# A hybrid decoder layer on one core: pair products taken from rows as loaded, the residual input loaded by feature, and a tile's preparation spread over more half-jobs

## The chip, the cores and the metric

The kernel runs on 1 core of one Trainium2 chip. The metric is the device time of one execution in microseconds (us), as the median of several runs of the same program. The text writes PE for TensorE, DVE for VectorE, ACT for ScalarE, POOL for GpSimd and SP for SyncE; PEld is the weight load that PE does beside its matmuls, and SPq in a row is SP's own sequencer.

## The reference

One inference step of a one-layer decoder, for a prompt of 1024 tokens and for 8 sequences of 4 sample tokens (32 rows), model width 1024, all float32:

```python
h = rmsnorm(x, g_mix); proj = h @ w_in                       # q|k|v, z, b, a, glu
qkv = silu(causal_depthwise_conv(qkv_full, w_short))         # 4 taps
q = l2norm(heads(q)); k = l2norm(heads(k))                   # 8 heads x 64
# chunks of 64 tokens: L = strict(k_beta k^T * decay), T = (1 + L)^-1
# u = T v_beta, w = T (k_beta e^gc), qk = (q k^T) * decay, then a scan over chunks
o, s_new = gated_delta_rule(q, k, v, g, beta, s0)
o = rmsnorm(o, g_o) * silu(heads(z))
cv = silu(group_layernorm(depthwise_conv31(glu)))            # 31 taps
x = x + concat([o, cv]) @ w_out
x = x + square(relu(rmsnorm(x, g_mlp) @ w_up)) @ w_down
x = x + (p_emb @ w_ple) * sigmoid(rmsnorm(x, g_ple) @ w_ple_gate)
y = rmsnorm(x, g_final)                                      # also: new states
```

## The kernel before, in words

The tokens are worked on in two halves: half 0 holds 512 prompt tokens in one piece, half 1 holds 512 prompt tokens and the 32 sample rows in two pieces of 256 and 288 columns. Activations lie by feature (128 features on the partitions, tokens along the free axis). Every large product is a list of **jobs** (plan, L82): one job makes one block of 128 output features. A weight block of up to 128x1024 is loaded by SP, ACT makes its high part (split_hi, L939) and DVE its low part (split_lo, L1656), three buffers deep, and PE does three matmuls for every 128 input features, high by high, low by high and high by low (L1318). The order of jobs is: input projections of half 0, those of half 1, then for half 0 the 8 `out` jobs, 8 groups of 4 `up` jobs and 8 short `down` jobs each, and 8 pairs of `gate` and `ple`; then the same for half 1. There the groups are longer.

Each job is issued in two **half-jobs**. `schedule` (L150) hangs every other piece of work behind one half-job as a stage, and every engine works through its own instructions strictly in that order; a stage of DVE that comes late holds up all that stands behind it on DVE, and PE waits for whatever it needs. The helper `adv(h, k)` goes forward from half-job h by about k units of a full half-job's PE time; the half-jobs of a `down` job in half 0 count half a unit.

The delta rule works on **tiles** of 128 tokens, t = 0..3 in half 0, 4..7 in half 1, t = 8 the sample rows. `prep` (L167) hangs five stages on half-jobs:

- `dk`: POOL makes products of gate logs and a triangle (`ug`, L893), PE turns them into decay exponents, ACT takes exp (Dm, L1114).
- `tok`: PE transposes the tile of q, k and v (`qt`, loaded from `qkv_dram`) to token rows (12 matmuls, L1406), ACT squares q and k (L1108), DVE sums the squares (L1858).
- `sc`: ACT makes the norms (L943, L1120, each after a table load), DVE five small scale factors (L1870 to L1874) and then evicts seven 128x512 products (L1878): tk[0..3], Kbe, Kd and Vb.
- `bk`: PE transposes tk[0..3] back to features (16 matmuls, L1419) and ACT copies them out (L1129) as KTl, RR twice, and QdT.
- `pr`: PE multiplies the chunks' keys with keys and queries (64 small matmuls, L1430), DVE masks the decays (L1885) and writes LQ (L1889), SP stores its key part to `lt_dram`.

After four tiles `lp` loads the pair matrices (Lp, L769), DVE inverts them by columns (L1903, L1904) and the scan over 8 chunks follows. Taps of the 31-wide convolution (`tap`, L1984) fill DVE between the stages, by a fill level that `conv` works out.

The residual input x comes in rows (xr, xrs; `load_rows`, L785 to L795, five loads issued together for each half): an `out` job ends with PE transposing 128x128 blocks of it into the job's PSUM accumulation (`residual`, L1294 to L1303), and ACT reads the PSUM three times (L1007 to L1009: xT, the input of the next product, and the square).

Of the kernel before, what the change touches and what calls it, by code (L numbers as in the profile page):

```python
# [13 lines left out]
P = 128  # L14
# [135 lines left out]
def schedule():  # L150
# [156 lines left out]
    put(max(scan_end, o0 - 4), "xr", 0)  # L307
# [7 lines left out]
    put(h, "dk", NT)  # L315
    put(h, "tok", NT)
    for what in ("sc", "bk", "pr"):
        h = adv(h)
        put(h, what, NT)
# [30 lines left out]
    put(o1 - 10, "xr", 1)  # L350
# [5 lines left out]
    conv(0, lambda p: half("ga", 0, p // 2 * 2 + 1) + 3, half("ga", 1, 2) - 2)  # L356
# [27 lines left out]
SEVEN = uses({"vec": 1, "abt": 1, "ge": 1, "dk": 1, "bk": 1, "uw": 1, "got": 1, "hq": 3})  # L384
# [41 lines left out]
def seg(t):  # L426
    return 0 if t < HT else 1
# [11 lines left out]
def build(nc, a, o):  # L439
    ctx = ExitStack()  # L440
    with ctx:
# [80 lines left out]
        xr = [at(MX, "xr0", [P, HT, D], off=12288), at(M0, "xr1", [P, HT, D], off=51200)]  # L522
        xrs = at(MX, "xrs", [NS, D], off=17408)
# [32 lines left out]
        cur[MX] += 4 * H * (P - C)  # L556
# [5 lines left out]
        prod = at(MX, "prod", [P, C * C])  # L562
        assert cur[MX] == 32768
# [1532 lines left out]
```

## Time and profile before

| | |
|---|---|
| median of 3 runs | 1711.07 us (1709.12 to 1714.03) |
| the profiled execution's own time | 1710.08 us |
| its span, first to last instruction | 1708.3 us |
| mean granted TensorE clock in it | 0.963 of full speed |
| PE, DVE, ACT, POOL busy | 92%, 57%, 43%, 3% |
| DMA, mean over the span | 90 GB/s |

The span is what the trace covers; 1.8 us of the execution lie around it. An engine's busy share is a mean over very different stretches: in some PE never stops, in others it waits for DVE. A row of the timeline or of the chain begins with its start and its length in us; `[6.60 <-DVE u_lo L1770]` behind it says how long the engine stood idle before it and what ended that. Matmuls are pipelined, so the lengths of two that follow each other overlap.

### The profile page before, as it was taken

Reading aid. Unit: us, or ns where it says so; the run is one execution under the profiler, and the core shown is the slowest. Engines: PE = TensorE matmul, PEld = TensorE weight load, DVE = VectorE, ACT = ScalarE, POOL = GpSimd, SP = SyncE. Lnnn points to the kernel's source line nnn. Section 1 sums busy time; section 2 is a strip of 40 time slices with the busy share of each in tenths; the row PEclk is TensorE's granted clock in tenths of the full one; section 3 lists DMA queues with packets and bytes.
Section 4 is the critical chain, followed back from the end, with each engine's and each line's share of the span. In section 5 each row is a group of like instructions: output and inputs, shape, how many; then the busy total and the mean of one; then the engine's idle time right before and its main releaser. Section 6 shows DMA issues by size and latency. Waiting matters only on the chain.

```text
span 1708.3 us, 27767 instructions
## 1 busy us (share of the span) xinstructions
PE 1570.2 (92%) x11576; PEld 1373.3 (80%) x11576; DVE 979.2 (57%) x1683; ACT 730.0 (43%) x1135; POOL 55.8 (3%) x68
## 2 busy tenths in 40 slices
PE   4898988999989997889999999889999999999987
PEld 2786778899868765767787877668899999999987
DVE  3765897787554565768855555654343434434543
ACT  5555634544446233434322226545542323324444
POOL 0000000000000030000000000000000000000000
PEclk8999989999999998989999999999999999999998
DMA  6345333232134142422331212242322323333322
GB/s 186 86 136 134 84 109 104 73 82 76 50 118 100 49 112 67 103 83 67 103 81 44 72 38 78 89 142 75 112 75 87 87 89 90 94 87 87 91 63 86
DMA packets 281025, 153.37 MB, mean 90 GB/s; under 512 B 36996, under 2 KB 272636, under 8 KB 280893
## 3 DMA queue, kind: packets, MB, share of 16 engines
q1 hardware_dynamic: 279879, 150.32, 31.0%
q8 instruction: 92, 1.51, 0.4%
q10 hardware_dynamic: 1022, 1.28, 0.3%
q14 instruction: 32, 0.26, 0.1%
HBM read 135.03 MB, written 16.97 MB: 89 GB/s over the span
## 4 chain that ended last, share of the span: by engine, by line
PE 72%; DVE 12%; ACT 7%; issue 4%; DMA 4%; ACTq 0%; SPq 0%; POOL 0%; DVEq 0%; POOLq 0%
PE ps L1318 59%; PE ps L1452 2%; PE ps L1486 2%; DVE w_lo L1656 2%; PE ps L1480 2%; DVE of L1984 2%; DVE tk L1878 1%; DVE Xp L1904 1%; ACT L943 1%; PE ps L1301 1%; DVE prod L1903 1%; PE ps L1442 1%; DMA qt<-qkv_dram 1%; ACT w_hi L939 1%; DMA qkv_dram<-yb 1%
## 5 line engine op out<-in xcount | busy, mean ns | idle before, releaser
L1656 DVE TENSOR_TENSOR w_lo<-w_raw,w_hi 128x1024 fp32r<-128x1024 f32 (+3 forms) x258 | 266.6, 1034 | 129.3 <-ACT w_hi L939 128.7
L1318 PE MATMUL ps<-hh_hi,w_hi 128*128 128x256 f32 (+1 forms) x960 | 318.8, 332 | 20.5 <-DVE w_lo L1656 14.7
L939 ACT ACTIVATE w_hi<-w_raw 128x1024 fp32r<-128x1024 f32 (+3 forms) x258 | 231.9, 901 | 247.0 <-DMA w_raw<-in_w_down 127.9
L1318 PE MATMUL ps<-hh_lo,w_hi 128*128 128x256 f32 (+1 forms) x960 | 313.2, 326 | 0.0
L1318 PE MATMUL ps<-hh_hi,w_lo 128*128 128x256 f32 (+1 forms) x960 | 312.7, 326 | 0.0
L1318 PE MATMUL ps<-u_hi,w_hi 128*128 128x512 f32 (+2 forms) x768 | 260.8, 340 | 28.0 <-DVE u_lo L1770 18.8
L1318 PE MATMUL ps<-u_lo,w_hi 128*128 128x512 f32 (+2 forms) x768 | 252.8, 329 | 0.0
L1318 PE MATMUL ps<-u_hi,w_lo 128*128 128x512 f32 (+2 forms) x768 | 252.2, 328 | 0.0
L1318 PE MATMUL ps<-hm_hi,w_hi 128*128 128x512 f32 (+5 forms) x600 | 206.8, 345 | 17.6 <-ACT yb L968 6.7
L1318 PEld LDWEIGHTS ps<-hh_hi,w_hi 128*128 128x128 f32 x960 | 183.1, 191 | 42.6 <-DVE w_lo L1656 23.5
L1318 PE MATMUL ps<-hm_hi,w_lo 128*128 128x512 f32 (+5 forms) x600 | 198.7, 331 | 0.0
L1318 PE MATMUL ps<-hm_lo,w_hi 128*128 128x512 f32 (+5 forms) x600 | 198.6, 331 | 0.0
L1318 PEld LDWEIGHTS ps<-hh_hi,w_lo 128*128 128x128 f32 x960 | 183.1, 191 | 13.9
L1318 PEld LDWEIGHTS ps<-hh_lo,w_hi 128*128 128x128 f32 x960 | 183.6, 191 | 13.1 <-issue 0.7
L1318 PEld LDWEIGHTS ps<-u_hi,w_hi 128*128 128x128 f32 x768 | 147.6, 192 | 46.9 <-DVE u_lo L1770 21.8
L1984 DVE SCALAR_TENSOR_TENSOR of<-gl,wdw,of 128x512 f32<-128x512 f32 x240 | 176.3, 778 | 0.9
L1318 PEld LDWEIGHTS ps<-u_hi,w_lo 128*128 128x128 f32 x768 | 147.4, 192 | 12.1
L1318 PEld LDWEIGHTS ps<-u_lo,w_hi 128*128 128x128 f32 x768 | 148.1, 193 | 11.1 <-issue 1.5
L1318 PEld LDWEIGHTS ps<-hm_hi,w_hi 128*128 128x128 f32 (+1 forms) x600 | 115.7, 193 | 32.3 <-issue 20.0
L1692 DVE TENSOR_TENSOR xT<-xT,ps 128x512 f32<-128x512 f32 (+2 forms) x128 | 71.6, 559 | 116.1 <-PE ps L1318 116.0
L1017 ACT ACTIVATE yb<-yb 128x256 f32<-128x256 f32 (+1 forms) x96 | 47.7, 497 | 202.1 <-DVE yb L1685 202.1
L1318 PEld LDWEIGHTS ps<-hm_lo,w_hi 128*128 128x128 f32 (+1 forms) x600 | 115.5, 193 | 11.3 <-issue 2.8
(274 smaller groups left out, 2113.7 us busy)
## 6 DMA issues: line engine op xcount, KB each, us to landing
w_raw<-in_w_up SPq DMA_DIRECT2D x64, 512.0 KB, 4.1
w_raw<-in_w_in SPq DMA_DIRECT2D x48, 512.0 KB, 4.2
w_raw<-in_w_down SPq DMA_DIRECT2D x64, 256.0 KB, 2.8
w_raw<-in_w_down SPq DMA_DIRECT2D x32, 512.0 KB, 3.8
w_raw<-in_w_out SPq DMA_DIRECT2D x16, 512.0 KB, 3.8
w_raw<-in_w_ple_gate SPq DMA_DIRECT2D x16, 512.0 KB, 3.8
qt<-qkv_dram SPq DMA_DIRECT2D x8, 768.0 KB, 5.1
xin<-in_x_prompt SPq DMA_DIRECT2D x8, 512.0 KB, 6.5
```

The costliest lines, as they stand in the source:

```text
L939: nc.scalar.activation(w_hi[job.slot][:, 0:job.kts, 0:job.m], w_raw[job.slot][:, 0:job.kts, 0:job.m], ACT.Copy).then_inc(w_hid, 1)
L943: ac.step(nc.scalar.activation(dst, src, ACT.Ln, **kw))
L1017: nc.scalar.activation(sg[:, lo:hi], yb[i % 2][:, lo:hi], ACT.Square).then_inc(u_sq, 1)
L1301: last = nc.tensor.matmul(dst[:, c0 - lo:c0 - lo + n], xr_of(t)[0:n, job.i * P:(job.i + 1) * P], ident[0:n, 0:n], start=False, stop=True, ...
L1318: last = nc.tensor.matmul(dst, wt[job.slot][:, k, 0:m], x[:, k, lo:hi], start=(i == 0 and n == 0), stop=(end and n == 2), skip_group_check ...
L1442: last = nc.tensor.matmul(ps[:, 7, h * HD:(h + 1) * HD], T, Vb[:, t % HT, h * HD:(h + 1) * HD], start=True, stop=True)
L1452: last = nc.tensor.matmul(ps[r, bank + par, q * HD:(q + 1) * HD], src[rows, q, r], S[rows, q, :], start=(first or q == 0), stop=first, ski ...
L1480: last = nc.tensor.matmul(ps[par * HD:(par + 1) * HD, 2, q * HD:(q + 1) * HD], Kd[r, t % HT, h * HD:(h + 1) * HD], Vn[r, h * HD:(h + 1) * ...
L1486: last = nc.tensor.matmul(ps[r, 4 + par, q * HD:(q + 1) * HD], LQ[r, t % HT, par * PR + q, 1, :], Vn[r, h * HD:(h + 1) * HD], start=False, ...
L1656: nc.vector.tensor_tensor(w_lo[job.slot][:, 0:job.kts, 0:job.m], w_raw[job.slot][:, 0:job.kts, 0:job.m], w_hi[job.slot][:, 0:job.kts, 0:jo ...
L1692: nc.vector.tensor_tensor(rows, rows, src, ALU.add).then_inc(freed(job, c), 1)
L1984: ins = nc.vector.scalar_tensor_tensor(out=rows, in0=gl[:, p, k:k + HALF], scalar=w, in1=rows, op0=ALU.mult, op1=ALU.add)
```

## The change

Five edits:

1. **Pair products from rows as loaded.** For the eight prompt tiles `pr` multiplies straight from `qt`, which already holds q and k by feature, without norms. So tk[0..2] and three of the four back transposes with their copies fall away; only QdT stays. The norms come back in elsewhere: POOL multiplies the mask by the keys' norms (two 128x128 operations a tile, `key_norms`), rows of the inverse get a rate each (one 128x1024 multiplication on DVE in each half; the rates go through PE, ACT and DRAM, stage `bl`), and the queries' norms go into the small factors of the gate norm (one small DVE operation more in `gsq` and one in `gno`). The pair products write PSUM banks 4 and 5 in place of 2 and 3. The sample tile keeps the old form.
2. **The residual by feature.** A further input, x transposed on the host, is loaded straight into xT: eight loads of 128x512 (128x544) in each half, hung on half-jobs 56, 58 to 70 and 287, 290 to 308, in place of five loads issued together. `residual` is gone. DVE adds the job's PSUM to xT (`take_rows`, 24 pieces), ACT reads xT twice in place of PSUM three times.
3. **Preparation further apart.** In half 0 `bk` and `pr` share one half-job, and the distance from tile to tile stays 4 units. In half 1 `sc` comes 2 units behind `tok`, `pr` and `bk` 2 behind `sc`, and the distance from tile to tile is 6 units; the inverse then begins at half-job 190 (187 before). For the sample tile `sc` moves one half-job further from `tok`, and all its later steps by one to three.
4. **Convolution of half 0 earlier.** Its last place is 6 half-jobs ahead of job ga 2 of half 1 in place of 2, and the taps are dealt out anew by `vector_load`; its norms (cm, cv, cr, cs) end at half-job 92 (98 before).
5. The loads of `qt` and `zt` wait for the pair products in place of the transposes, and `prod` is a quarter as large.

The core of the diff:

```diff
-    def prep(t, h, rest=1.0):
+    def prep(t, h, period=4.0):
         put(h, "dk", t)
         put(h, "tok", t)
...
+        n = adv(h, 1.0 if t < HT else 2.0)
+        put(n, "sc", t)
+        if t < NT:
+            n = adv(n, 1.0 if t < HT else 2.0)
+            put(n, "pr", t)
+            if t % HT == HT - 1:
+                put(n, "bl", t // HT)
+            put(n, "bk", t)
+            return adv(h, period)
...
-    put(max(scan_end, o0 - 4), "xr", 0)
+    for k in range(KT):
+        put(half("z", 1, 0) + 4 + 2 * k, "xr", 0, k)
...
         if t == HT:
-            h = adv(h, 2.5)
+            h = adv(h, 4.0)
         loads = adv(h)
-        h = prep(t, h, 2.0)
+        h = prep(t, h, 6.0)
...
-    put(o1 - 10, "xr", 1)
+    for k in range(KT):
+        put(done + 3 + 3 * k, "xr", 1, k)
...
-    conv(0, lambda p: half("ga", 0, p // 2 * 2 + 1) + 3, half("ga", 1, 2) - 2)
+    conv(0, lambda p: half("ga", 0, p // 2 * 2 + 1) + 3, half("ga", 1, 2) - 6)
...
             def load_pairs(s):
+                sp.wait_ge(rate_st, 16 * (s + 1))
+                sp.dma_start(rates[:, :], rate_dram[s].rearrange("m (b c) -> (m b) c", c=C)).then_inc(lt_ld, 16)
...
-            def load_rows(s):
+            def load_rows(s, k):
...
-                for t in TILES[s]:
-                    dst = xr[s][:, t % HT, :] if t < NT else xrs[:, :]
-                    sp.dma_start(dst, rows_of(a["x_prompt"][0], a["x_sample"], t)).then_inc(ld_xr[s], 16)
+                sp.dma_start(xT[s][:, k, :], a["x_by_feature"][k * P:(k + 1) * P, HALF * s:HALF * s + TS[s]]).then_inc(ld_xr[s], 16)
...
+            def key_norms(t):
+                n = PREP[t]
+                if t < NT:
+                    pool.wait_ge(n_r, n + 1)
+                    wait(pool, d_msk, n - 1)
+                    for r in range(2):
+                        rk = rn[:, t, H:2 * H].rearrange("p (q r) -> p r q", r=2)[:, r, :]
+                        last = nc.gpsimd.tensor_tensor(trk[n % 2][:, r * PR:(r + 1) * PR, :], bc(rk, 2, C), bc(consts["tri"][:, :], 1, PR), ALU.mult)
+                    last.then_inc(d_rk, 1)
...
-                done(act, job, c)
-                nc.scalar.activation(xT[s][:, m, lo:hi], src, ACT.Copy)
-                nc.scalar.activation(hh[s][0][:, m, lo:hi], src, ACT.Copy, scale=gains[:, 1, m:m + 1]).then_inc(h_hi, 1)
-                nc.scalar.activation(square_of(s, 0, m, c), src, ACT.Square).then_inc(freed(job, c), 1)
+                gone(act, job, c)
+                nc.scalar.activation(hh[s][0][:, m, lo:hi], xT[s][:, m, lo:hi], ACT.Copy, scale=gains[:, 1, m:m + 1]).then_inc(h_hi, 1)
+                nc.scalar.activation(square_of(s, 0, m, c), xT[s][:, m, lo:hi], ACT.Square).then_inc(sq_out, 1)
...
                 if ks[-1] == job.kts - 1:
-                    if job.kind == "out":
-                        last = residual(job, c)
...
             def back(t):
-                for k, (bank, big) in enumerate(((5, 1), (7, 2), (2, 4), (3, 6))):
+                for k, bank, big in ((3, 7, 2),) if t < NT else ((0, 5, 1), (1, 7, 2), (2, 2, 4), (3, 3, 6)):
...
             def pairs(t):
-                pe.wait_ge(g_ev, 3 * n + 3)
+                pe.wait_ge(g_big, scaled_in(n) + (1 if t < NT else 7))
...
+                            keys = rows_in[rows, PR + q, r] if t < NT else KTl[rows, q, r]
+                            both = rows_in[rows, q:q + PR + 1:PR, r] if t < NT else RR[rows, q, :, r]
...
+            def take_rows(job, c):
                 src, lo, hi = out_of(job, c)
                 rows = xT[job.s][:, job.i, lo:hi]
+                if job.kind == "out":
+                    dve.wait_ge(ld_xr[job.s], 16 * (job.i + 1))
                 done(dve, job, c)
                 nc.vector.tensor_tensor(rows, rows, src, ALU.add).then_inc(freed(job, c), 1)
...
+                    plan = ((4, Vb[:, v, :], beta[:, t, :]), (2, tk[3], egc[:, t, :]), (3, Kbe[:, v, :], sc[:, 1]), (3, Kd[:, v, :], sc[:, 2]))
...
             def inverse_columns(s, first, end):
-                dve.wait_ge(lt_ld, 16 * (s + 1))
+                dve.wait_ge(lt_ld, 32 * (s + 1))
+                if first == 0:
+                    step(nc.vector.tensor_tensor(Lm, Lm, bc(rates[:, :], 1, C), ALU.mult))
```

Three places show what the schedule makes of it. In the rows the numbers behind a name are buffers, and line numbers of the changed kernel are its own. First PE in half 0, at tile 0, between two half-jobs of the projections. Before:

```order
L1318 MATMUL ps<-hm_hi,w_lo_87 128x512
L1419 MATMUL ps<-c_ident,tk_155 128x128 x4
L1419 MATMUL ps<-c_ident,tk_156 128x128 x4
L1419 MATMUL ps<-c_ident,tk_157 128x128 x4
L1419 MATMUL ps<-c_ident,tk_158 128x128 x4
L1318 MATMUL ps<-hm_hi,w_hi_90 128x512
```

and with the change:

```order
L1345 MATMUL ps<-hm_hi,w_lo_88 128x512
L1467 MATMUL ps<-qt_143 32x64 x32
L1445 MATMUL ps<-c_ident,tk_156 128x128 x4
L1345 MATMUL ps<-hm_hi,w_hi_91 128x512
L1345 MATMUL ps<-hm_lo,w_hi_91 128x512
```

The pair products have come one half-job forward, and of the four groups of transposes one is left. The second place is DVE at tile 4, the first of half 1, where an `up` group ends and the `down` jobs begin; the first `down` matmuls wait for the two u_lo of the group's last job. Before, `sc` of tile 4 begins right behind the first of them, and its evictions stand ahead of the second:

```order
L1878 TENSOR_TENSOR tk_157<-ps,scb 128x512
L1878 TENSOR_TENSOR tk_158<-ps,scb 128x512
L1878 TENSOR_TENSOR Kbe<-ps,scb 128x512
L1878 TENSOR_TENSOR Kd<-ps,scb 128x512
L1878 TENSOR_TENSOR Vb<-ps,beta 128x512
L1685 SCALAR_TENSOR_TENSOR yb_96<-ps,rs 128x512
L1656 TENSOR_TENSOR w_lo_85<-w_raw_82,w_hi_88 128x512
L1770 TENSOR_TENSOR u_lo<-yb_97,u_hi 128x512
```

With the change tile 4's `sc` stands among the `down` jobs, and what follows it is the low part of a weight block:

```order
L1917 TENSOR_TENSOR scb<-scb 128x8
L1918 TENSOR_TENSOR scb<-scb,egc 128x8
L1929 TENSOR_TENSOR Vb<-ps,beta 128x512
L1929 TENSOR_TENSOR tk_156<-ps,egc 128x512
L1929 TENSOR_TENSOR Kbe<-ps,scb 128x512
L1929 TENSOR_TENSOR Kd<-ps,scb 128x512
L1730 TENSOR_TENSOR xT_111<-xT_111,ps 128x512
L1692 TENSOR_TENSOR w_lo_87<-w_raw_84,w_hi_90 128x512
```

The third place is DVE at tile 6 with the change, at the end of the next `up` group (before, tile 6's `sc` stood in the middle of that group):

```order
L1918 TENSOR_TENSOR scb<-scb,egc 128x8
L1929 TENSOR_TENSOR Vb<-ps,beta 128x512
L1929 TENSOR_TENSOR tk_156<-ps,egc 128x512
L1929 TENSOR_TENSOR Kbe<-ps,scb 128x512
L1929 TENSOR_TENSOR Kd<-ps,scb 128x512
L1721 SCALAR_TENSOR_TENSOR yb_97<-ps,rs 128x512
L1692 TENSOR_TENSOR w_lo_86<-w_raw_83,w_hi_89 128x512
L1808 TENSOR_TENSOR u_lo<-yb_98,u_hi 128x512
```

So the order that tile 4 had, with `sc` between the last two u_lo of a group, is now tile 6's, with four evictions in it in place of seven.

## Rows read from the trace of the kernel before

**Rows 1.** The page: busy time by engine, and the chain that ended last by engine.

```profile
PE 1570.2 (92%) x11576; PEld 1373.3 (80%) x11576; DVE 979.2 (57%) x1683; ACT 730.0 (43%) x1135; POOL 55.8 (3%) x68
...
PE 72%; DVE 12%; ACT 7%; issue 4%; DMA 4%; ACTq 0%; SPq 0%; POOL 0%; DVEq 0%; POOLq 0%
```

**Rows 2.** Windows, tiles 0 to 3 and tiles 4 to 7: length, busy time, PEclk, DMA.

```profile
130.00:205.00 75.00, 66.83 (x535) 51.47 (x534) 50.51 (x88) 46.97 (x59) 3.36 (x6) 1.00 0.44 112
640.00:800.00 160.00, 133.07 (x820) 104.61 (x819) 110.38 (x197) 60.02 (x90) 4.46 (x6) 0.89 0.29 79
```

**Rows 3.** Windows of L1301 alone, `out` jobs of half 0 and half 1.

```profile
488.00:552.00 64.00, 9.30 (x64) 9.30 (x64) 0.98 0.33 88
1155.00:1240.00 85.00, 12.39 (x80) 10.92 (x80) 0.98 0.30 94
```

**Rows 4.** The chain in the `out` jobs of half 0, two jobs apart: start, length, what.

```profile
521.99 5.51 PE ps L1318 x24
...
534.80 5.51 PE ps L1318 x24
```

**Rows 5.** Groups by line: DVE's addition onto xT in the `down` jobs.

```profile
L1692 DVE TENSOR_TENSOR xT<-xT,ps 128x512 f32<-128x512 f32 (+2 forms) x128 | 71.6, 559 | 116.1 <-PE ps L1318 116.0
```

**Rows 6.** Timeline of PE at tile 0, `bk` and `pr`, with the next half-job's first matmul.

```profile
147.89 1.10 PE L1419 MATMUL ps<-c_ident,tk 128*128 128x128 f32 x8
...
149.53 0.66 PE L1419 MATMUL ps<-c_ident,tk 128*128 128x128 f32 x4 [0.54 <-DVE tk L1878]
...
150.72 0.66 PE L1419 MATMUL ps<-c_ident,tk 128*128 128x128 f32 x4 [0.54 <-DVE Kd L1878]
...
154.07 0.86 PE L1430 MATMUL ps<-RR,KTl 64*32 64x64 f32 x64
```

**Rows 7.** Waits of PE from 640 to 800 us: in total, times, longest.

```profile
PE ps L1318 <- DVE u_lo L1770: 12.9, 3, 6.6
PE ps L1318 <- DVE w_lo L1656: 9.0, 4, 4.1
PE ps L1406 <- DMA qt<-qkv_dram: 5.0, 1, 5.0
```

**Rows 8.** Timeline at tile 4: `sc` on DVE, and the first `down` matmul.

```profile
645.30 1.88 DVE L1878 TENSOR_TENSOR tk<-ps,scb 128x512 f32<-128x512 f32 x3
...
651.67 0.80 PE L1318 MATMUL ps<-u_hi,w_hi 128*128 128x512 f32 x1 [6.60 <-DVE u_lo L1770]
```

**Rows 9.** Waits of PE from 455 to 500 us, ahead of the `out` jobs.

```profile
PE ps L1318 <- DVE op_lo L2024: 4.5, 2, 3.1
```

**Rows 10.** The chain behind the loads of xr in half 1.

```profile
1133.28 5.79 PE ps L1318 x24
...
1142.06 9.03 DMA w_raw<-in_w_ple_gate
...
1153.48 7.31 PE ps L1318 x24
```

**Rows 11.** DMA issues: a gate weight's load, and a load of 256 KB.

```profile
w_raw<-in_w_ple_gate SPq DMA_DIRECT2D x16, 512.0 KB, 3.8
...
zt<-zs_dram SPq DMA_DIRECT2D x8, 256.0 KB, 2.9
```

**Rows 12.** PE's longest wait from 205 to 290 us, in half 0's inverse.

```profile
PE ps L1318 <- ACT yb L985: 4.7, 1, 4.7
```

**Rows 13.** Timeline of DVE in the inverse: a 128x1024 operation.

```profile
230.24 1.22 DVE L1656 TENSOR_TENSOR w_lo<-w_raw,w_hi 128x1024 fp32r<-128x1024 f32 x1
```

**Rows 14.** Timeline: two taps on DVE alone, two beside POOL, and POOL's `ug` pair.

```profile
156.56 1.41 DVE L1984 SCALAR_TENSOR_TENSOR of<-gl,wdw,of 128x512 f32<-128x512 f32 x2
...
316.71 1.76 DVE L1984 SCALAR_TENSOR_TENSOR of<-gl,wdw,of 128x512 f32<-128x512 f32 x2
316.94 0.99 POOL L905 TENSOR_TENSOR Sd<-S,gld 128x256 f32<-128x256 f32 x1 [10.99 <-DVE S L1923]
...
638.97 0.76 POOL L893 TENSOR_TENSOR ug<-gg,c_tri 128x128 f32<-128x128 f32 x2 [23.36 <-PE ps L1386]
```

More of the change, by code:

```diff
@@ L241, in vector_load @@
             if (job, c) in EVICT[h]:
-                work += part * {"ga": 1, "up": 1, "down": 1, "gate": 1, "ple": 2}.get(job.kind, 0)
+                work += part * {"ga": 1, "out": 1, "up": 1, "down": 1, "gate": 1, "ple": 2}.get(job.kind, 0)
             else:
                 work += part * {"out": 2, "up": 1, "down": 2 * job.last, "ple": 1, "qkv": 3.5 * job.n * (c == job.n - 1)}.get(job.kind, 0)
-        own = {"tok": 1.6, "sc": 7, "pr": 1.5, "c1": .7, "c2": .6, "gsq": .9, "gno": .9, "got": 1, "cm": 1, "cs": 1, "dc": 5, "op": 1,
+        own = {"tok": 1.6, "sc": 5, "pr": 1.7, "c1": .7, "c2": .6, "gsq": .9, "gno": .9, "got": 1, "cm": 1, "cs": 1, "dc": 5, "op": 1,
                "sp": .9, "tap": 1, "pe": .6, "inv0": 2.4}
@@ L314, in schedule @@
     put(h, "s0")
[L315 to L319, printed above, removed]
+    h = prep(NT, h)
     put(h, "zt", NT)
@@ L555, in build @@
         ug = at(MX, "ug", [P, H, C])
-        cur[MX] += 4 * H * (P - C)
+        trk = [at(MX, f"trk{n}", [P, H, C]) for n in range(2)]
+        rateT = at(MX, "rateT", [H * HT, P])
+        rates = at(MX, "rates", [P, C])
+        cur[MX] = 30720
         Dm = [at(MX, f"Dm{n}", [P, H, C]) for n in range(2)]
@@ L1292, in ready @@
                     pe.wait_ge(b6, SIX[("pe", TILES[s][-1])] + 1)
-            def residual(job, c):
-                dst, lo, hi = out_of(job, c)
-                pe.wait_ge(ld_xr[job.s], 16 * len(TILES[job.s]))
-                for t in TILES[job.s]:
-                    c0, n = local(t)
-                    if lo <= c0 < hi:
-                        last = nc.tensor.matmul(dst[:, c0 - lo:c0 - lo + n], xr_of(t)[0:n, job.i * P:(job.i + 1) * P], ident[0:n, 0:n],
-                                                start=False, stop=True, skip_group_check=True)
-                return last
             def multiply(job, c, ks):
@@ L1709, in take_ple @@
                 nc.vector.tensor_tensor(rows, rows, sg[:, lo:hi], ALU.add).then_inc(x_new, 1)
-            take = {"ga": take_ga, "up": take_up, "down": take_down, "gate": take_gate, "ple": take_ple}
+            take = {"ga": take_ga, "out": take_rows, "up": take_up, "down": take_rows, "gate": take_gate, "ple": take_ple}
             def short_conv(job, c):
@@ L1762, in finish_out @@
                 low_rows(job.s, 0, job.i, c)
-                gone(dve, job, c)
+                dve.wait_ge(sq_out, lo_count(job.s, 0, job.i, c) - (KT if job.s else 0))
                 add_square(job.s, 0, job.i, c)
@@ L2087 @@
         arrays[f"in_{name}"] = np.ascontiguousarray(inputs[name])
+    rows = np.concatenate([inputs["x_prompt"][0], inputs["x_sample"].reshape(NS, D)], axis=0)
+    arrays["in_x_by_feature"] = np.ascontiguousarray(rows.T)
     arrays["in_consts"] = shape_constants()
```

157 lines of the change are left out of this document (98 added, 59 removed).

## The prediction, made before the changed kernel was run

> **What bounds the kernel now.** I read the page first. PE is busy 92% of the span and the chain that ended last lies 72% on PE and 12% on DVE [rows 1]. So work taken from PE's own sequence counts in full nearly everywhere, and work taken from another engine counts only where PE waits. Next come the windows [rows 2]. From 130 to 205 us PE is busy 66.8 of 75 us, from 640 to 800 us only 133.1 of 160, and there the granted clock is 0.89: its lower level, half speed (1.2 GHz), sets in behind each longer stop. These two stretches are the preparation of tiles 0 to 3 and 4 to 7. The waits of the second [rows 7] name three causes: the low part u_lo 12.9 us, the low part w_lo 9.0, the load of qt 5.0. The first two are DVE's, and the timeline says why [rows 8]: at tile 4 the evictions of `sc` stand ahead of the last u_lo, and the first `down` matmul comes 6.60 us late. Outside these stretches the change touches the `out` jobs, where transposes of x lie between the jobs [rows 3, 4], and the load burst ahead of the `out` jobs of half 1 [rows 10].
>
> **The terms, against the profiled execution's 1710.1 us.** "About what a measurement of this kernel can tell from no change" is 0.3%, here 5 us.
>
> *Residual off PE.* In half 0 two `out` jobs are 12.81 us apart, 6.40 each, of which 5.51 is the job's own matmuls [rows 4]: 0.89 a job goes, 7.1 for eight. The 64 transposes are busy 9.30 us there and the 80 of half 1 12.39 [rows 3]; what is over 7.1 is overlap with the matmuls around them and, at a clock of 0.98, some half-speed time that counts in full, so I take 8.0 for half 0 and by the same ratio 10.7 for half 1. Together **-18.7**. In their place DVE adds the PSUM onto xT, 0.56 us a piece [rows 5], 24 pieces; an `out` job leaves DVE 5.5 us and it has a split, a low part and a sum to do in it, some 3 us, so this costs nothing while PE is the bound. If that cover were gone it would be 24 x 0.56 = 13. ACT loses one of three reads a piece, which nobody waits for.
>
> *Preparation, tiles 0 to 3.* At tile 0 PE spends 147.89 to 151.13 in `bk`, two waits of 0.54 included, and 0.8 in `pr` (0.86, overlapped a little) [rows 6], together 4.0. Now it is the 0.8 and four transposes (half of the 1.10 for eight), 1.35; Vb, which frees bank 4, is the first eviction and is done as PE arrives. Gain 2.7 a tile, and a wait of 0.3 more at tiles 2 and 3: **-11.4**, taken as -11. The wait for qt at tile 1 stays: its load is issued in step with PE.
>
> *Entry of the `out` jobs.* Four convolution norms leave the stretch ahead of them, with their matmuls on PE and their table loads on ACT; PE waits 4.5 us for op_lo there [rows 9]. The samples' taps (`dc`) still stand ahead of op_lo, so I take about half, **-2.5** (0 to -5).
>
> *Preparation, tiles 4 to 7.* Work: 12 transposes a tile and less overlap lost, 1.4 each, **-5.7**. Waits: of 26.9 us [rows 7], 5.0 for qt stay, and 4.8 at places that aren't touched. The rest, 17, is tile 4's 6.6 and w_lo and u_lo behind `sc` of tiles 5 to 7. Three evictions go, 1.88 [rows 8]; `sc` of tile 4 moves among `down` jobs, where w_lo has less room, so its 6.6 becomes some 2; tile 5's falls away in an `up` group, tile 7's 4.1 becomes 2.2. But `sc` of tile 6 now stands where tile 4's stood, between the last two u_lo. It saves the 1.88 and loses as much, since its norms begin on ACT only after the job's u_hi: 6.5 again, where 3 was. So 17 becomes 11, -6. Half-clock time behind the stops goes with them, 1 or so. Together **-12** (-5 to -24).
>
> *The load burst of half 1.* The xr loads were issued at once; the gate weight behind them took 9.03 us [rows 10] where the median is 3.8 [rows 11], 5.2 late, and PE's next 24 matmuls took 7.31 in place of 5.79, half clock at their start. That is 6.7; a little of it was a wait for DVE that stays: **-6.3**.
>
> *The 16 new loads.* No row shows them. From below: they are hidden, 0. From above: each holds the queue 2.9 us, as a load of 256 KB does [rows 11], and PE pays it all, 46. The nearest row is the burst itself: 9 such quarters of a megabyte cost 6.7, so 0.75 each or 12. These are spread, one in two or three half-jobs, with weight loads issued three jobs ahead, so I take a quarter of that, **+3**, and keep 0 and 12.
>
> *Sample tile.* `sc` and what follows come one to three half-jobs later, and its evictions now meet the first `down` jobs. 0 if they fit, 6.6 if it goes as at tile 4 [rows 8]; its u_lo has more room: **+2**, the small additions to `gsq` and `gno`, two of them waited for, included.
>
> *Inverse of half 0.* DVE is full there and PE waits 4.7 us behind it [rows 12]. The multiplication by the rates is 128x1024, like the split at 1.22 [rows 13], and the rates' load comes ahead of Lp's, some 0.4; one more tap is dealt in, 0.7: **+2.2** (0.5 to 4). In half 1 DVE has room and it is hidden.
>
> *POOL's key norms.* POOL is idle, 3%. But two taps beside a POOL operation take 1.76 us in place of 1.41, and POOL's own takes 0.99 [rows 14], so each delays the other. The new pair, like that of `ug`, is 0.76 alone and falls on the small factors at the head of each `sc`. Paid as the taps pay, 0.35, at the three tiles where DVE is late, it is 1; I leave it in the rounding. The Trainium skill ("SBUF — State Buffer", section "Who interferes with whom") speaks against this edit more strongly: a DVE instruction with two SBUF inputs and a GpSimd instruction that reads SBUF lock each other out for the whole instruction. The trace agrees in kind, not in size. By that rule the price is 3 x 0.76 = 2.3 and the sum comes to 1669.
>
> Sum: -18.7 - 11 - 2.5 - 12 - 6.3 + 3 + 2 + 2.2 = -43.3, so 1710.1 - 43.3 = **1667 us**. The profiled execution lies 1.0 under the median, well inside the runs' own spread.
>
> **Rivals.** *Half 1 gives nothing back.* The stops at DVE only change their tile, and the half-clock stretches with them; w_lo behind `sc` of tiles 4 and 7 waits as now. For it: tile 6 takes tile 4's place, order for order. Then the -12 is the work alone, -5.7, less a new stop of some 6: about **1679**. *The stops vanish.* DVE has 3 evictions a tile less and two units between steps, u_lo and w_lo come in time and the clock holds: -24 in place of -12, and the loads are hidden: **1652**. Against it: 6.60 came from order, not from load, DVE being busy only 110 of 160 us. *Residual hidden.* If DVE or ACT, not PE, becomes the bound of the `out` jobs, of the 18.7 only some 5 is left: **1680**; against it the 3 of 5.5 us. *Slower: the one queue.* The new loads fall among spills of qkv and the weights of half 0's last groups. PE stops for a weight when three jobs' lead is used up. If each of 16 holds PE for 2.9 and pays half clock behind each stop, 1.5 as in rows 10, that is 70 in place of 3: 1667 + 67 = **1734**. It decides from (43.3 + 3 + 5) / 16 = 3.2 us a load on; the burst's 0.75 speaks against it. *The change isn't what it says* (pair products still behind the transposes, for instance): the order shows the transposes gone, so under 1 in 100.
>
> **How the numbers follow.** Forecast 0.54 (own range 1658 to 1676), half 1 gives nothing back 0.17, the stops vanish 0.13, residual hidden 0.08, slower 0.05, the rest small losses that together undo the gain 0.03. The range takes in the three faster rivals with the bounds of the loads, 1648 to 1688. Faster by over 0.3%: the first four together, 0.92; no difference 0.03; slower 0.05.
>
> **What would show it.** Right: the chain without PE L1301 and `out` jobs of half 0 5.5 us apart; `bk` and `pr` together 1.4 us of PE; gate weights of half 1 at 3.8 us; from 640 to 800 us one long u_lo wait, at tile 6, and w_lo waits of 2 at most. Wrong: PE waiting for xT's additions or for hh_lo in the `out` jobs; w_raw loads above 6 us beside the new loads; several u_lo waits above 4; a wait over 6 in the inverse of half 0.

## The result, and the profile after

The changed kernel takes **1668.62 us** (1666.47 to 1670.79, 4 runs) beside 1711.53 us (1709.12 to 1714.03, 4 runs) for the kernel before: a ratio of 0.9753, 95% interval 0.9734 to 0.9772, so faster. The forecast was 1667 in a range of 1648 to 1688. The profiled execution took 1667.82 us, 42.3 under that of before. The total came out nearly as summed, but two of its largest terms missed in opposite directions, so that part of its closeness is luck.

The page of the changed kernel, busy time by engine and the chain by engine, against [rows 1]:

```profile
PE 1535.3 (92%) x11338; PEld 1342.7 (81%) x11338; DVE 983.2 (59%) x1709; ACT 710.6 (43%) x1088; POOL 61.9 (4%) x84
...
PE 70%; DVE 15%; ACT 7%; issue 4%; DMA 3%; ACTq 0%; POOL 0%; SPq 0%; DVEq 0%
```

PE is busy 34.9 us less, at the same busy share. The two preparation stretches, windows as in [rows 2]:

```profile
130.00:205.00 75.00, 66.85 (x570) 52.15 (x569) 55.65 (x95) 43.80 (x53) 5.60 (x15) 0.96 0.43 112
640.00:800.00 160.00, 138.02 (x860) 106.22 (x861) 118.80 (x211) 66.58 (x91) 9.76 (x16) 0.96 0.34 93
```

In the second PE is busy 5 us longer of the same 160, and the granted clock went from 0.89 to 0.96. In the first the clock fell from 1.00 to 0.96: a surprise, followed up below. PE's waits from 640 to 800 us, against [rows 7]:

```profile
PE ps L1345 <- DVE u_lo L1808: 10.3, 3, 7.2
PE ps L1432 <- DMA qt<-qkv_dram: 6.3, 1, 6.3
PE ps L1345 <- DVE w_lo L1692: 5.7, 8, 1.6
```

There is one long stop for u_lo left and no long one for w_lo. The long one stands at tile 6 (timeline, DVE and then PE):

```profile
704.33 0.17 DVE L1910 TENSOR_TENSOR scb<-rn,ekd 128x8 f32<-128x8 f32 x1 [1.98 <-ACT rn L1150]
...
710.82 0.80 PE L1345 MATMUL ps<-u_hi,w_hi 128*128 128x512 f32 x1 [7.23 <-DVE u_lo L1808]
```

The chain in the `out` jobs of half 0, against [rows 4]: no transposes of x between the jobs, and the last five follow each other without a gap (120 matmuls in 27.47 us, 5.49 a job).

```profile
500.56 5.51 PE ps L1345 x24
...
506.29 2.75 PE ps L1345 x12
509.05 0.22 PE ps L1611 x2
509.27 27.47 PE ps L1345 x120
```

DMA issues, against [rows 11] (the last number is the median us from issue to landing): the gate weights and the new loads of x.

```profile
w_raw<-in_w_ple_gate SPq DMA_DIRECT2D x16, 512.0 KB, 4.1
...
xT<-in_x_by_feature SPq DMA_DIRECT2D x8, 272.0 KB, 3.3
...
xT<-in_x_by_feature SPq DMA_DIRECT2D x8, 256.0 KB, 4.4
```

To give every term its own time, I counted the job matmuls out in the timelines and took the time from the start of one half-job's first matmul to that of another's. In these stretches the kernels do the same work of the jobs, so a difference beyond the scatter is the edit's. Times in us; the columns behind "after" are experiments, told below:

| stretch (half-jobs) | before | after | e1 | e2 | e4 | e5 | e6 | e9 | e12 |
|---|---|---|---|---|---|---|---|---|---|
| tiles 0 to 3 (34–50) | 71.7 | 66.8 | 72.7 | 67.5 | 60.6 | 67.8 | 65.4 | 65.5 | 58.5 |
| inverse, scan of half 0 (50–100) | 260.7 | 264.5 | 260.8 | 264.3 | 264.2 | 264.3 | 265.5 | 262.7 | 264.0 |
| `out` of half 0 (100–116) | 63.4 | 54.8 | 56.9 | 54.9 | 57.3 | 54.8 | 57.6 | 55.0 | 54.9 |
| sample tile (116–143) | 86.0 | 90.5 | 85.9 | 87.8 | 90.3 | 87.8 | 91.8 | 89.8 | 93.0 |
| tiles 4 to 7 (143–188) | 135.2 | 118.6 | 135.0 | 134.6 | 111.1 | 126.3 | 117.1 | 141.8 | 109.9 |
| inverse, scan of half 1 (188–287) | 284.8 | 284.3 | 287.1 | 294.7 | 284.0 | 287.0 | 294.2 | 294.9 | 286.0 |

Further on, 330 to 340 (the load burst) goes from 23.8 to 18.2, the `out` jobs of half 1 (340 to 356) from 64.9 to 52.4, and 356 to 500 from 430.5 to 429.4.

How far such a difference can be trusted shows where kernels have the same program. Tiles 0 to 3 are alike in the changed kernel, e2, e5, e6 and e9, and take 65.4 to 67.8: PE's waits are the same there, but more or fewer matmuls run at half speed. The `out` jobs of half 0 are alike in all columns from "after" on but e1, and take 57.3 and 57.6 in e4 and e6 beside some 54.9, again with the same waits, at a granted clock of 0.91 beside 0.97. In these two stretches one difference of under some 2.5 us shows nothing by itself. Tiles 4 to 7 scatter less: e7, e8 and e11, which don't touch them, take 118.3 to 118.6.

### The profile page after: what moved, and what is told of

It reads as the page before. It is cut to its first block, busy times and chain, and to the rows that moved or that the text cites. A ratio compares the mean times of both kernels' runs of the same rounds, so it can differ in the third digit from the quotient of the medians.

```text
span 1666.0 us, 27343 instructions
## 1 busy us (share of the span) xinstructions
PE 1535.3 (92%) x11338; PEld 1342.7 (81%) x11338; DVE 983.2 (59%) x1709; ACT 710.6 (43%) x1088; POOL 61.9 (4%) x84
## 4 chain that ended last, share of the span: by engine, by line
PE 70%; DVE 15%; ACT 7%; issue 4%; DMA 3%; ACTq 0%; POOL 0%; SPq 0%; DVEq 0%
PE ps L1345 58%; DVE of L2046 3%; PE ps L1488 2%; DVE w_lo L1692 2%; PE ps L1522 2%; PE ps L1516 2%; DVE Xp L1961 1%; DVE prod L1960 1%; DMA qt<-qkv_dram 1%; PE ps L1478 1%; ACT L972 1%; DVE yb L1721 1%; DVE u_lo L1808 1%; PE ps L1569 1%; DMA Lp<-lt_dram 1%
## 5 line engine op out<-in xcount | busy, mean ns | idle before, releaser
L1345 PE MATMUL ps<-u_hi,w_hi 128*128 128x512 f32 (+2 forms) x768 | 256.5, 334 | 25.0 <-DVE u_lo L1808 18.7
L1345 PE MATMUL ps<-u_lo,w_hi 128*128 128x512 f32 (+2 forms) x768 | 249.3, 325 | 0.0
L1345 PEld LDWEIGHTS ps<-hh_hi,w_hi 128*128 128x128 f32 x960 | 182.8, 190 | 38.3 <-DVE w_lo L1692 18.7
L2046 DVE SCALAR_TENSOR_TENSOR of<-gl,wdw,of 128x512 f32<-128x512 f32 x240 | 172.9, 763 | 1.1
L1730 DVE TENSOR_TENSOR xT<-xT,ps 128x512 f32<-128x512 f32 (+2 forms) x152 | 84.0, 553 | 131.4 <-PE ps L1345 131.0
```

The lines of the kernel that those rows point to most:

```text
L1345: last = nc.tensor.matmul(dst, wt[job.slot][:, k, 0:m], x[:, k, lo:hi], start=(i == 0 and n == 0), stop=(end and n == 2))
L1730: nc.vector.tensor_tensor(rows, rows, src, ALU.add).then_inc(freed(job, c), 1)
L2046: ins = nc.vector.scalar_tensor_tensor(out=rows, in0=gl[:, p, k:k + HALF], scalar=w, in1=rows, op0=ALU.mult, op1=ALU.add)
```

## The experiments

Each kernel was timed against the kernel before on its chip (medians there 1712 to 1715 us), so kernels are compared by ratio: 0.001 is 1.7 us. "Against the changed kernel" is the ratio less 0.9753, times 1711.5. The names in the headings are those of the table.

### e1: the residual alone

The kernel before with the second edit alone; its core:

```diff
-                    if job.kind == "out":
-                        last = residual(job, c)
...
-    put(max(scan_end, o0 - 4), "xr", 0)
+    for k in range(KT):
+        put(half("z", 1, 0) + 4 + 2 * k, "xr", 0, k)
```

> The kernel before with the residual edit alone (loads by feature, addition on DVE, no transposes). Theory (the terms add): the out jobs of half 0 lose 7 to 9 us, those of half 1 12 to 13, the load burst ahead of them 5 to 6, and nothing else moves: 25 to 27 us under the kernel before, near 1685. Rival (the new loads cost what the sum put on them, 3 us or more, or the edits help each other): under 21 us, near 1692 or above.

1688.22 us, ratio 0.9866 (0.9846 to 0.9886): -24.3 us by the medians, a little under the 25 to 27 of the theory and above the rival's 21. The `out` jobs give 6.5 and 12.5, the burst 5.6; the others move by 2.3 or less. So more than half of the whole gain is this one edit; about 19 us belong to the others.

### e2, e5, e9: the old distances

The pair edit kept, the distances of the steps in half 1 as before. e2 sets both back, e5 that of `sc` alone (the first hunk):

```diff
-        n = adv(h, 1.0 if t < HT else 2.0)
+        n = adv(h)
         put(n, "sc", t)
...
-            h = adv(h, 4.0)
+            h = adv(h, 2.5)
```

> The changed kernel with the old distances in half 1: sc one unit behind tok in place of two, first tile 2.5 units behind its load in place of 4. Theory (where sc falls against the end of an up group decides, not the distance): sc of tile 6 falls into the middle of an up group and its wait of 7.2 us with the half clock behind it goes, sc of tile 5 falls among down jobs and waits 1.5 to 3 there: 4 to 9 us faster than the changed kernel. Rival (the wider spacing is what saves the waits): the stalls of tiles 4 and 5 come back, 5 to 10 us slower than the changed kernel.

1691.21 us, ratio 0.9883 (0.9859 to 0.9908): 22 us slower than the changed kernel, and no faster than e1. The theory fell; the rival held in direction, at more than twice its 5 to 10. **With the old distances the pair edit brings nothing in tiles 4 to 7**: they take 134.6 us, where before took 135.2. Another 10 us are lost between half-jobs 188 and 287. Windows of tiles 4 to 7: before, after, e2.

```profile
627.00:762.00 135.00, 111.97 (x749) 88.20 (x748) 90.56 (x153) 50.84 (x78) 5.22 (x8) 0.89 0.31 83
```
```profile
621.00:741.00 120.00, 100.47 (x720) 78.39 (x718) 82.76 (x142) 48.15 (x72) 7.02 (x15) 0.94 0.37 100
```
```profile
619.00:754.00 135.00, 106.04 (x708) 81.68 (x707) 87.32 (x148) 48.41 (x71) 8.21 (x16) 0.91 0.33 88
```

In e2 PE is busy 5.9 us less than before in the same 135: the work did go. It came back as waits; before, then e2:

```profile
PE ps L1318 <- DVE u_lo L1770: 9.2, 2, 6.6
PE ps L1318 <- DVE w_lo L1656: 7.9, 3, 4.1
```
```profile
PE ps L1345 <- DVE w_lo L1692: 10.0, 5, 3.5
PE ps L1345 <- DVE u_lo L1808: 7.5, 2, 3.8
PE ps L1432 <- DMA qt<-qkv_dram: 6.2, 1, 6.2
PE ps L1532 <- DVE onr L2001: 2.8, 1, 2.8
PE ps L1467 <- DVE Vb L1929: 2.1, 1, 2.1
```

The low parts together take 17.5 us of waits in e2 and 17.1 before, beside 12.7 in the changed kernel; new against before are the gate norm onr of the sample tile, Vb, and 1.2 us more for qt. What DVE waits for in that stretch suggests a reason, first e2, then the changed kernel:

```profile
DVE scb L1910 <- ACT rn L1150: 8.3, 4, 3.4
```
```profile
DVE scb L1910 <- ACT rn L1150: 2.5, 2, 2.0
```

Between a tile's token rows and its small factors lies a chain in series: squares on ACT, their sum on DVE, two table loads and the norms on ACT. With one unit between `tok` and `sc` DVE stands still at all four tiles, and what stands behind it on DVE is late; with two units it stands still at two of the four. That this chain is the cause is argued and not shown: with one unit too, e5 has 5.0 us of these waits and the kernel before 4.5. Nor do the runs separate the distance from the place. The first hunk moves `sc` of the sample tile as well, so that all steps of half 1 shift against the `up` and `down` groups: `tok` of tile 4 hangs on half-job 146 before, 151 in the changed kernel, 147 in e2 and 149 in e5.

> The changed kernel with only the distance from tok to sc back at one unit in half 1; the first tile stays 4 units behind its load. The kernel with both at the old values was 22.7 us slower than the changed one. If the distance is what pays (the norms are then ready when DVE arrives), this kernel is 15 to 22 us slower than the changed one, near 1686. If the place of the first tile pays, it is within 6 us of it, near 1671.

1677.20 us, ratio 0.9791 (0.9755 to 0.9828): 6.5 us slower, with an interval that overlaps that of the changed kernel a little. The stretch says it more sharply: 126.3 us for tiles 4 to 7, about halfway between 118.6 and 134.6. Neither number was met. And the 7.7 us that e5 loses here are hardly waits: PE is idle 20.6 us of the stretch in e5 and 19.5 in the changed kernel, but 38 of its job matmuls run at half speed beside 9, which is 5.8 us at 0.2 each. In e5 the waits are five stops of 2.8 to 6.2 us; in the changed kernel they are two of 6.3 and 7.2, and three of 1.5 to 1.7 behind which the granted clock stays at 1.00. The step from e5 to e2, where the first tile comes earlier still, is idle time, 8.4 us. For the sample tile the wider distance is a loss, though: 90.5 us with it and 87.8 without (in all kernels with the pair edit, 90.3 to 93.1 with it and 87.8 to 89.8 without).

The taps are dealt out anew whenever stages move, so e2 might have tested the dealing. e9 is e2 with the 124 taps of half 1 held at the changed kernel's places (PLACES lists them):

```diff
+        if s == 1:
+            places = [h for h, n in PLACES for _ in range(n)]
```

> The kernel with both old distances again (22.7 us slower than the changed one), but with the taps of half 1 held at the 124 places that the changed kernel gives them, so that only the preparation moves. Theory (10 of the 22.7 us come from taps and convolution norms that were dealt out anew, up to 120 half-jobs later): the loss up to half-job 188, 13 us, stays, that behind it goes: near 1682. Rival (the distances themselves cost all of it): near 1691.

1698.41 us, ratio 0.9914 (0.9897 to 0.993): slower still by 5, where the theory wanted it faster than e2. Tiles 4 to 7 take 141.8 us; PE waits 12.6 us for w_lo there. That taps dealt for one set of distances collide with another is the likely reason; the old distances cost their time either way. Why e2 and e9 both lose another 10 us between half-jobs 188 and 287 isn't explained: about 4 of it is idle time of PE, the granted clock is 0.95 there beside 0.98 in the changed kernel, and holding the taps doesn't remove it.

### e3: POOL's products later

```diff
-                    pool.wait_ge(n_r, n + 1)
+                    pool.wait_ge(g_big, scaled_in(n) + 1)
```

`key_norms` starts behind Vb in place of the norms, so it no longer runs beside the small factors.

> The changed kernel with POOL's key norms waiting for the eviction of Vb in place of the norms, so that they no longer run beside the small factors of sc. Theory (POOL and DVE shut each other out, 0.6 us a tile): the small factors from L1914 on take 0.16 us each again, Vb comes 0.6 us earlier, PE's waits for Vb at tiles 2 and 3 fall from 1.0 and 1.1 to about 0.4, the long wait at tile 6 from 7.2 to 6.6: 2 to 4 us faster in all. Rival (the small factors are long for another reason): they stay at 0.33 to 0.40 us and the time stays within 1 us.

1668.31 us, ratio 0.9747 (0.9731 to 0.9763): no difference that can be told, where the theory had 2 to 4 us. Locally all is as it said. Tile 2 in the changed kernel:

```profile
182.06 0.77 POOL L922 TENSOR_TENSOR trk<-rn,c_tri 128x128 f32<-128x128 f32 x2 [15.15 <-ACT rn L1150]
...
182.48 0.37 DVE L1916 TENSOR_TENSOR scb<-rn,beta 128x8 f32<-128x8 f32 x1
...
182.89 0.33 DVE L1917 TENSOR_TENSOR scb<-scb 128x8 f32<-128x8 f32 x1
...
184.07 0.86 PE L1467 MATMUL ps<-qt 64*32 64x64 f32 x64 [0.97 <-DVE Vb L1929]
```

and in e3:

```profile
182.69 0.16 DVE L1916 TENSOR_TENSOR scb<-rn,beta 128x8 f32<-128x8 f32 x1
...
183.91 0.86 PE L1467 MATMUL ps<-qt 64*32 64x64 f32 x64 [0.37 <-DVE Vb L1929]
```

The factors are back to 0.16, PE's wait for Vb falls from 0.97 to 0.37, and the stop at tile 6 from 7.23 to 6.63: 0.60 a tile. Over eight tiles, of which few are late, that drowns in the measurement.

### e4: qt one step earlier

The second tile's qt is loaded one half-job behind the first's, not when it is used:

```diff
-        put(h if t < 2 else loads, "qt", t)
+        if t != 1:
+            put(h if t < 2 else loads, "qt", t)
         if t == 0:
+            put(h + 1, "qt", 1)
```

and the same for tiles 4 and 5.

> The changed kernel with the loads of qt for tiles 1 and 5 issued one half-job behind those of tiles 0 and 4, in place of in the same half-job that uses them. Theory (the wait is the load's own length, its issue being bound to PE's half-job): both waits, 4.3 and 6.3 us, go, with some 2 us of half clock behind the second: 11 to 13 us faster than the changed kernel. Rival (the queue is full there, and the load lands as late when issued earlier, or another load pays): under 5 us.

1654.43 us, ratio 0.9664 (0.9649 to 0.9679): 15 us faster than the changed kernel, more than the 11 to 13 of the theory and the largest single step of the study after e1. Tiles 0 to 3 gain 6.2 us, tiles 4 to 7 gain 7.5, and the `out` jobs of half 0 give 2.5 back in the profiled execution. The waits of the changed kernel and of e4 from 130 to 205 us:

```profile
PE ps L1432 <- DMA qt<-qkv_dram: 5.2, 2, 4.3
```
```profile
PE ps L1436 <- DMA qt<-qkv_dram: 1.0, 1, 1.0
```

The wait falls by 4.2, of which Vb, which PE now meets earlier, takes 0.6 back. The rest is the clock: in the changed kernel 13 of that window's job matmuls start 0.43 us apart, at half speed, against 0.23 otherwise, and in e4 none does: 13 x 0.2 = 2.6. The number varies, though: e8 and e9, with the waits of the changed kernel there, have 4 and 5.

### e6, e10: `sc` of tile 6 later

e6 moves it past the last u_lo of the group, to take the 7.23 us stop away:

```diff
+        if HT <= t < NT and JOBS[n // 2].kind == "up" and JOBS[n // 2 + 1].kind == "down" and n % 2:
+            n += 2
         put(n, "sc", t)
```

> The changed kernel with sc of tile 6 moved by two half-jobs, from ahead of the last u_lo of an up group to behind it, among the down jobs. Theory (DVE's order there costs the 7.2 us, and half clock behind it 1.5 to 3): the u_lo wait falls to about 2, a wait of 1.6 for w_lo comes in, as at tiles 4 and 7: 5 to 8 us faster than the changed kernel. Rival (DVE is full there and the same work is late at the next place): within 2 us.

1680.08 us, ratio 0.9807 (0.9779 to 0.9835): 9 us slower, where the theory had 5 to 8 faster. Tiles 4 to 7 win 1.5 (the stop is 3.45, but w_lo pays 2.15). The loss lies 100 half-jobs away, at 264 to 288, where the convolution's last taps and its norms (from half-job 279 on, 266 in the changed kernel) now meet the low parts: of 10.4 us there 4.2 are idle time of PE, and the granted clock is 0.92 beside 1.00. Windows there of e6, of the changed kernel and of e10, which is e6 with the taps held as in e9:

```profile
980.00:990.00 10.00, 8.27 (x58) 6.82 (x59) 2.64 (x5) 2.06 (x4) 0.61 (x1) 0.64 0.09 26
```
```profile
980.00:990.00 10.00, 10.00 (x109) 8.40 (x108) 4.36 (x7) 4.97 (x7) 0.62 (x1) 1.00 0.18 54
```
```profile
980.00:990.00 10.00, 10.00 (x104) 8.07 (x100) 4.36 (x8) 4.97 (x7) 0.61 (x1) 1.00 0.18 54
```

> The kernel with sc of tile 6 two half-jobs later (11.5 us slower than the changed one), with the taps held at the changed kernel's places. Theory (moving sc itself gives 1 us, the loss came from the taps dealt out anew at half-jobs 264 to 281): 1666 to 1669. Rival (the loss belongs to the place of sc): near 1680.

1668.22 us, ratio 0.9742 (0.9716 to 0.9768): the loss is gone and with it the whole difference to the changed kernel. So e6's loss was the dealing of the taps. And moving the stop wins next to nothing by itself (tiles 4 to 7 take 117.7, 0.9 less), because it comes back at the low parts of the weights; waits of e10 there:

```profile
PE ps L1352 <- DVE w_lo L1699: 8.2, 5, 4.4
...
PE ps L1352 <- DVE u_lo L1815: 3.1, 2, 1.7
```

In the changed kernel these two were 3.8 and 8.9.

### e7: the new loads in one burst

The eight loads of each half at the old place, and every addition waits for all eight:

```diff
-        put(half("z", 1, 0) + 4 + 2 * k, "xr", 0, k)
+        put(max(scan_end, o0 - 4), "xr", 0, k)
...
-        put(done + 3 + 3 * k, "xr", 1, k)
+        put(o1 - 10, "xr", 1, k)
...
-                    dve.wait_ge(ld_xr[job.s], 16 * (job.i + 1))
+                    dve.wait_ge(ld_xr[job.s], 16 * KT)
```

> The changed kernel with the eight loads of each half issued at one half-job each, where the row loads of before stood (97 and 330). Theory (the burst delays the gate weight behind it, the spread loads delay nothing): half 1 loses the 5.6 us that the change gained there, half 0 nothing much: 5 to 7 us slower than the changed kernel. Rival (the spread loads do cost what the sum put on them, or more): the same or faster than the changed kernel, since 3 us come back at half-jobs 56 to 70 and 287 to 308.

1674.36 us, ratio 0.979 (0.9751 to 0.9829): 6 us slower, with a wide interval. The chain of e7 has the burst of [rows 10] again, and 330 to 340 takes 24.8 us:

```profile
1119.50 7.97 DMA w_raw<-in_w_ple_gate
...
1129.86 8.07 PE ps L1345 x24
```

So the spreading of the loads, not their form, is what the burst's term is made of.

### e8: the addition twice

```diff
+                if job.kind == "out":
+                    step(nc.vector.tensor_tensor(rows, rows, src, ALU.add))
                 nc.vector.tensor_tensor(rows, rows, src, ALU.add).then_inc(freed(job, c), 1)
```

> The changed kernel with DVE's addition onto xT done twice in the out jobs (so x plus twice the product: another result), 24 more operations of 0.56 us, 13 us in all. Theory (out jobs leave DVE room: about 3 of 5.5 us used): within 2 us of the changed kernel. Rival (DVE is near the bound there): 8 to 13 us slower.

1667.61 us, ratio 0.974 (0.9714 to 0.9766): no difference. The additional pieces are there, and PE is what ends the idle time ahead of them (group by line of e8):

```profile
L1731 DVE TENSOR_TENSOR xT<-xT,ps 128x512 f32<-128x512 f32 (+2 forms) x24 | 12.4, 517 | 15.4 <-PE ps L1345 15.4
```

12.4 us more on DVE cost nothing, so the 24 additions of the change don't either.

### e11: without the rates

```diff
-                if first == 0:
-                    step(nc.vector.tensor_tensor(Lm, Lm, bc(rates[:, :], 1, C), ALU.mult))
```

> The changed kernel without the multiplication of the pair matrices' rows by the rates (another result; the loads stay). Theory (DVE is full in the inverse of half 0, and what is added there is paid by PE): the wait of 4.8 us for w_lo at half-job 54 falls by the 1.2 us of the operation, in all 1 to 3 us faster. Rival (DVE catches up): within 0.5 us.

1668.28 us, ratio 0.9733 (0.9713 to 0.9754). The wait for w_lo in half 0's inverse falls from 4.8 to 3.6, the 1.2 us of the operation, but the total differs by less than the measurement tells. Inconclusive: 1.2 us is under its resolution.

### e12: what the runs pointed to

e4 and e3 together, and Lp loaded one half-job earlier:

```diff
-        put(h, "lp", s)
+        put(h - 1, "lp", s)
```

> Three edits on the changed kernel together: the loads of qt for tiles 1 and 5 one half-job behind those of tiles 0 and 4 (alone 1654.4 us), POOL's key norms behind the eviction of Vb (alone 1668.3), and the load of Lp one half-job earlier than the inverse's first stage. If they add, the third taking the 1.9 us that DVE waits for Lp in half 0: 1650 to 1653. Rival (Lp's load only meets another in the queue, or SP stands longer for the last store and weights come late): 1654 or above.

**1650.42 us** (1648.98 to 1654.82, 4 runs), ratio 0.9632 (0.9614 to 0.965): 21 us faster than the changed kernel and 63 faster than before. The waits of PE in half 0's inverse fall; first the changed kernel, then e12:

```profile
PE ps L1345 <- DVE w_lo L1692: 4.8, 1, 4.8
PE ps L1345 <- ACT yb L1014: 4.7, 1, 4.7
```
```profile
PE ps L1349 <- DVE w_lo L1696: 3.9, 2, 2.8
PE ps L1349 <- ACT yb L1018: 3.5, 1, 3.5
```

e4's 15 us are most of it; the 5 beyond are at the edge of what the intervals tell (its profiled execution, 1654.82, is the longest of the four). The stretch 50 to 100 hardly moves (264.5 to 264.0), so the earlier Lp isn't shown to pay.

## Why the prediction was right, and where it was not

Term by term, in us; "measured" is the difference of the two profiled executions in the stretches of the table:

| term | predicted | measured |
|---|---|---|
| residual off PE | -18.7 | -19.0 (e1) |
| entry of the `out` jobs | -2.5 | -2.2 (after less e1, 100–116) |
| load burst | -6.3 | -5.6 |
| the 16 new loads | +3 | within the scatter (287–330: +1.1 in e1, -0.4 in the changed kernel) |
| tiles 0 to 3 | -11 | **-4.9** |
| tiles 4 to 7 | -12 | **-16.6** |
| sample tile | +2 | +4.5 |
| inverse of half 0 | +2.2 | +3.8 (50–100) |

The stretches not named gain another 2 us and make up the 42.3. That the sum was met is partly luck: tiles 0 to 3 missed by 6.1 one way, tiles 4 to 7 by 4.6 the other.

**Residual, loads, cover.** Right in step and size. e1 shows the first (6.5 and 12.5 for the two halves, where 8.0 and 10.7 were summed), e7 the burst, and e8 the cover on DVE that the cost of nothing rested on. "Residual hidden" fell. So did "slower: the one queue": gate weights land in 4.1 us, and the weights issued while the new loads run in 5.9 at most, not above 6; and 287 to 330, where those of half 1 are issued, takes 93.1 in e1, 92.0 before and 91.5 after.

**Entry of the `out` jobs.** The number is met by luck. The term was half of PE's wait for op_lo, and that wait fell from 4.5 to 3.7 us only. The rest of the 2.2 is the clock, granted at 0.97 in that stretch and at 0.94 in e1; e4 and e6, with the same edit and the same waits, ran there at 0.91 and are no faster than e1 (57.3 and 57.6).

**Tiles 0 to 3.** The step that failed is "Vb, which frees bank 4, is the first eviction and is done as PE arrives", and with it "the wait for qt at tile 1 stays". Tile 0 of the changed kernel on PE, against [rows 6]: the work is 1.2 us, as short as forecast, but behind a wait.

```profile
148.24 0.86 PE L1467 MATMUL ps<-qt 64*32 64x64 f32 x64 [0.35 <-DVE Vb L1929]
149.03 0.66 PE L1445 MATMUL ps<-c_ident,tk 128*128 128x128 f32 x4
149.44 0.48 PE L1345 MATMUL ps<-hm_hi,w_hi 128*128 128x512 f32 x1
```

Vb makes PE wait 2.5 in three tiles, and rateT 0.4. At tile 1:

```profile
160.02 1.96 PE L1432 MATMUL ps<-c_ident,qt 128*128 128x128 f32 x12 [4.26 <-DMA qt<-qkv_dram]
```

Before:

```profile
161.41 1.53 PE L1406 MATMUL ps<-c_ident,qt 128*128 128x128 f32 x12 [2.95 <-DMA qt<-qkv_dram]
```

The load was issued with its use, PE now came sooner, and the wait grew from 2.95 to 4.26. Behind the longer stop the clock fell to half speed, which it had not done before: the 12 transposes took 1.96 in place of 1.53, and six job matmuls 0.43 in place of 0.23 each, 1.6 together; at tile 3 seven more followed the waits for Vb (1.14) and rateT, 1.4. With 2.5, 0.4 and 1.3 these sum to 7.2, about what is missing (6.1). By these figures 4.3 of it are behind Vb and rateT and 2.9 behind qt; the 1.4 at tile 3 comes and goes, for e6, e8 and e9 have the same waits there and no half speed. e4, without the long wait for qt, gains 11.1 against before, but that it equals the predicted 11 is chance: the forecast had left 2.95 of that wait in place, and e4 still waits 3.1 for Vb.

**Tiles 4 to 7.** The picture was right row by row: tile 4's stop gone, one long wait for u_lo at tile 6 (6.5 predicted, 7.23 found), w_lo's waits under 2. The sum was mis-sized in the step "half-clock time behind the stops goes with them, 1 or so". In the windows of e2's section PE is idle 23.0 us before and 19.5 after, so the waits gave 3.5, not 6. But PE's busy time fell by 11.5, twice the 5.7 of the work (that of the changed kernel is 1.4 us longer than its stretch, hence 15.0 here and 16.6 in the table). Of the job matmuls there, 38 ran at half speed before and 9 after; at 0.2 us each that is 5.8. And the forecast priced the work by itself: e2 shows that its 5.7 turn into waits where the distances stay. "The stops vanish" did not come either; e4 comes near its number at 111.1, but by qt's wait: those for u_lo, 8.9, are still there.

**Sample tile.** The term was there, its price too low and its mechanism wrong: `sc` does not meet the first `down` jobs, which begin at half-job 124. One half-job further from `tok`, at 120, it falls on ACT behind the u_hi of an `up` job, and ACT waits for DVE's yb before it can begin the norms. DVE then waits for the norms and PE for the first evictions. By e5 this is 2.7 of the 4.5.

```profile
547.62 0.64 ACT L1045 ACTIVATE yb<-yb 128x512 f32<-128x512 f32 x1 [3.10 <-DVE yb L1721]
...
552.09 0.15 DVE L1910 TENSOR_TENSOR scb<-rn,ekd 32x8 f32<-32x8 f32 x1 [3.38 <-ACT rn L1150]
...
553.44 1.23 PE L1445 MATMUL ps<-c_ident,tk 32*128 32x32 f32 x8 [2.86 <-DVE tk L1929]
```

**Inverse.** The multiplication is as predicted. DVE waits for Lp ahead of it; it did so before too, so that the rates' load adds 0.5, near the 0.4 of the sum. Before, then after:

```profile
223.18 0.19 DVE L1903 TENSOR_TENSOR prod<-Xp,Lp 128x31 f32<-128x31 f32 x1 [1.37 <-DMA Lp<-lt_dram]
```
```profile
219.50 1.23 DVE L1956 TENSOR_TENSOR Lp<-Lp,rates 128x1024 f32<-128x1024 f32 x1 [1.88 <-DMA Lp<-lt_dram]
```

How the 3.8 divide among this, the convolution's earlier norms and the taps stays open; e11 can't resolve its 1.2, and kernels that are alike there lie between 262.7 and 265.5 us.

**POOL.** My own price was 0.35 a tile. The Trainium skill ("SBUF — State Buffer", section "Who interferes with whom") has a DVE instruction with two SBUF inputs and a GpSimd one that reads SBUF lock each other out for the whole instruction. POOL's pair is 0.76 long here, and e3 measured 0.60 a tile, nearer the rule. Left in the rounding it did no harm to the sum.

## What to carry to other kernels

When PE is the bound, work taken off it pays in full only where the engines that feed it are early; elsewhere it turns into waits (e2 against before). So look at the steps that hang on a chain across engines (here squares, sums, table loads, norms), and give them distance before, or with, the removal of work. Count the stops and not only their sum, since each can bring half-speed time of its own (e5). Look for loads that are issued at the place of their use: once the engine ahead gets faster, such a load becomes the longest stop, and the half-speed stretch behind it counts as well. Where filler work is dealt out automatically, hold it fixed in an experiment or look for the loss far from the edit.

## What the hardware showed that was not expected

- A stop of PE can cost as much again in clock, and its length alone doesn't say whether it will. At tile 1 a stop of 2.95 us left the granted clock at 1.00; one of 3.04 in e1, the same program there, was followed by transposes of 2.82 in place of 1.53 us and a granted clock of 0.84 over ten us; one of 4.26 by job matmuls 0.43 apart (1.2 GHz) until 164.3 us and 0.83 from 160 to 170. At tiles 4 to 7 the same effect (granted clock 0.89 to 0.94 in the windows under e2) is 5.8 of 16.6 us gained.
- Small DVE operations of 128x8 take 0.33 to 0.40 us beside POOL's 128x128 products (three of a run of six, 0.60 us in all) and 0.16 to 0.17 when POOL stands aside (e3): the effect on a chain of tiny operations is larger in proportion than on the taps of [rows 14].
